# Seven block products for the value half of the second feed-forward, in 18 pairs of tiles

## The reference

```python
def conv_ffn(x, prev, w_up, conv_w, conv_b, w_down):
    L = x.shape[1]
    up = x @ w_up                                # 1024 -> 2 x 2816
    u, val = up[..., :D_FF], up[..., D_FF:]
    u_pad = jnp.concatenate([prev.astype(u.dtype), u], axis=1)
    c = conv_b
    for j in range(CONV_W):
        c = c + conv_w[j] * u_pad[:, j:j + L]
    h = jax.nn.gelu(c, approximate=True) * val
    return h @ w_down, u_pad[:, -(CONV_W - 1):]  # 2816 -> 1024
```

## Time and profile before

| what | value |
|---|---|
| runs | 2580.8, 2582.04, 2585.12 us |
| profiled execution | 2581.35 us, of which the span is 2579.5 us |
| TensorE busy | 2452.5 us (95%), 15399 matmuls |
| VectorE busy | 1614.0 us (63%) |
| ScalarE busy | 1149.6 us (45%) |
| GpSimd busy | 44.0 us (2%), DMA issues only |
| granted TensorE clock, mean | 0.988 of full |

### The profile page before, as it was taken

One profiled execution on the slowest core, in us unless ns is written; L12 is line 12 of the kernel. 1 busy time (PEld: TensorE's weight loads), 2 busy tenths in 40 slices (PEclk: granted clock), 3 DMA queues, 4 the chain that ended last, 5 costly groups with the idle time before them and its releaser, 6 DMA issues. The chain is left out here.

```text
span 2579.5 us, 37702 instructions
## 1 busy us (share of the span) xinstructions
PE 2452.5 (95%) x15399; PEld 2142.2 (83%) x15399; DVE 1614.0 (63%) x2922; ACT 1149.6 (45%) x1822; POOL 44.0 (2%) x66
## 2 busy tenths in 40 slices
PE   7999999989999999999998999889999999999997
PEld 4777988877888889999996677767788889999996
DVE  5667576675765556665656655665766556655556
ACT  4655454554343334343336666664344333423333
POOL 0000000000000000000000000000000000000000
PEclk9999999999999999999999999989999999999998
DMA  4222223323433322422323242222332323332322
GB/s 159 66 67 90 82 85 102 125 100 96 153 104 123 102 90 92 138 82 90 109 77 106 83 130 63 80 75 83 111 131 92 104 92 98 99 116 82 97 85 97
DMA packets 83592, 255.18 MB, mean 99 GB/s; under 512 B 12963, under 2 KB 30540, under 8 KB 81484
## 3 DMA queue, kind: packets, MB, share of 16 engines
q1 hardware_dynamic: 64348, 202.45, 25.0%
q0 software_dynamic: 5792, 28.05, 3.4%
q10 hardware_dynamic: 13280, 22.28, 2.6%
HBM read 225.93 MB, written 26.74 MB: 98 GB/s over the span
## 5 line engine op out<-in xcount | busy, mean ns | idle before, releaser
L447 PE MATMUL banks<-act_hi,w_lo 128*128 128x272 f32 (+1 forms) x2952 | 973.4, 330 | 15.7 <-DVE act_lo L2301 6.7
L447 PE MATMUL banks<-act_hi,w_hi 128*128 128x272 f32 (+1 forms) x2952 | 960.2, 325 | 0.0
L447 PE MATMUL banks<-act_lo,w_hi 128*128 128x272 f32 (+1 forms) x2952 | 958.3, 325 | 0.0
L425 ACT ACTIVATE w_hi<-w_raw 128x1024 fp32r<-128x1024 f32 x366 | 380.8, 1055 | 690.8 <-PE banks L470 487.2
L430 DVE TENSOR_TENSOR w_lo<-w_raw,w_hi 128x1024 fp32r<-128x1024 f32 x366 | 442.9, 1222 | 365.4 <-ACT w_hi L425 365.0
L447 PEld LDWEIGHTS banks<-act_hi,w_lo 128*128 128x128 f32 x2952 | 558.7, 189 | 75.4 <-issue 20.6
L447 PEld LDWEIGHTS banks<-act_lo,w_hi 128*128 128x128 f32 x2952 | 559.4, 190 | 43.2 <-issue 1.7
L447 PEld LDWEIGHTS banks<-act_hi,w_hi 128*128 128x128 f32 x2952 | 558.2, 189 | 43.8
L482 DVE TENSOR_TENSOR acc<-acc,banks 128x272 f32<-128x272 f32 (+1 forms) x624 | 314.7, 518 | 190.8 <-PE banks L470 187.3
L470 PE MATMUL banks<-h_hi,w_lo 128*128 128x272 f32 (+1 forms) x1056 | 345.3, 327 | 22.2 <-DVE acc L482 12.8
L470 PE MATMUL banks<-h_hi,w_hi 128*128 128x272 f32 (+1 forms) x1056 | 343.4, 325 | 0.0
(11 more groups left out here) (242 smaller groups left out, 2581.2 us busy)
## 6 DMA issues: line engine op xcount, KB each, us to landing
w_raw<-wall SPq DMA_DIRECT2D x366, 512.0 KB, 3.6
normed<-h_scratch POOLq DMA_DIRECT2D x20, 352.0 KB, 4.2
h_scratch<-acc POOLq DMA_DIRECT2D x3, 2176.0 KB, 7.8
h_scratch<-acc POOLq DMA_DIRECT2D x3, 2048.0 KB, 7.6
gstates<-state ACTq DMA_DIRECT2D x4, 1024.0 KB, 6.4
gla_s<-gstates ACTq DMA_DIRECT2D x4, 1024.0 KB, 6.8
bias<-bias_scratch ACTq DMA_DIRECT2D x28, 128.0 KB, 2.6
bias_scratch<-bias_rows ACTq DMA_DIRECT2D x8, 383.0 KB
```

Source lines behind the costliest of these rows:

```text
L425: nc.scalar.activation(WH[:, b % RING], WR[:, b % RAW], ACT.Copy).then_inc(w_hi, 1)
L447: last = nc.tensor.matmul(PS[:, bank, 0:n], w, a[X][:, k, o:o + n], start=(k == 0 and first), stop=(k == KT - 1 and w is wh and a is AH))
```

## The change

For f = 2 and 3 and each group g >= 2 (tiles 4 to 21, nine pairs each, 18 in all) the value half of the two tiles is computed together as a product of 2 x 2 blocks by Winograd's form of Strassen's scheme: the outputs are two tiles by two halves of the tokens (256 or 272 columns each), the sum runs over two halves of the features (KH = 4 blocks each). Instead of eight block products there are seven (`pe_products`), each of 12 matmuls of 256 or 272 columns.

- **Weights.** A pair has eight names in the list: u, u, `va`, `vs`, `vb`, `v4` and two downs. `va` and `vb` are loaded, each one half of the features of both tiles; `vs` (two sums, full size) and `v4` (one sum, half size) are made by GpSimd from them (`gp_three_sums`, `gp_fourth_sum`, four additions or subtractions of 128 x 512 per pair). `va` and `vs` are rounded after the third sum. So ScalarE and VectorE handle 7.5 blocks a pair where there were 6; loads stay 6.
- **Activation sums.** Four sums and differences of quarters of the activations are made once per half by GpSimd (`gp_act_sums`: eight instructions of 128 x 4 x 256 or 272, after the attention's last downs for f=2, after the last product of f=2 for f=3). ScalarE rounds them (`sums_hi`, four) and VectorE takes their rests (`sums_lo`, four) in tile 3, ahead of the round behind `val` and ahead of `product`, respectively.
- **Outputs.** ScalarE copies product 1 out of PSUM, VectorE makes seven additions and subtractions (`read_products`: `early`, `even`, `odd_tile`), then multiplies both tiles in SBUF by the gelu.
- **Order.** In an even tile t >= 4 TensorE does `u` and at once the downs of the group before, in an odd one `u` and the seven products. VectorE makes the even tile's convolution, a weight rest and up to two norm steps between the additions of the downs.
- **Waits and tables.** `u` of an even tile waits for the seventh read of the pair before; `u` of tile 0 of f=3 for the last multiply of f=2. `Root` and the steps behind it come later by two tiles and more (tables `DVE_SEVEN`, `DVE_AMID`, `ACT_SEVEN`). The result stores of tile 8 (f=3) now come ahead of the gelu of an even tile that is followed by the downs. Some semaphores are merged.

```diff
+SEVEN = (2, 3)
+def seven(f, g):
+    return f in SEVEN and g >= 2
...
+            pe.wait_ge(w_lo, BLK["va", f, g] + 1)
+            product("va", 1, own(AH, 0, 0), own(AL, 0, 0), 2)
+            pe.wait_ge(t_lo, 4 * SEVEN.index(f) + 4)
+            product("va", 0, made(TH, 0), made(TL, 0), 3)
+            pe.wait_ge(w_lo, BLK["vs", f, g] + 1)
+            pe.wait_ge(u_ev, TILE[f, odd, 0] if X else TILE[f, odd - 1, 0])
+            product("vs", 1, made(TH, 1), made(TL, 1), 0)
+            pe.wait_ge(u_ev, TILE[f, odd, c - 1])
+            product("vs", 0, made(TH, 2), made(TL, 2), 1)
+            pe.wait_ge(w_lo, BLK["vb", f, g] + 1)
+            pe.wait_ge(vp_read, 8 * N - 7)
+            product("vb", 1, own(AH, 1, 0), own(AL, 1, 0), 2)
+            pe.wait_ge(vp_read, 8 * N - 6)
+            product("vb", 0, made(TH, 3), made(TL, 3), 0)
+            pe.wait_ge(w_lo, BLK["v4", f, g] + 1)
+            pe.wait_ge(vp_read, 8 * N - 5)
+            product("v4", 0, own(AH, 1, 1), own(AL, 1, 1), 3)
...
+            if t % 2 == 0 and seven(f, t // 2 - 1):
+                pe.wait_ge(vp_read, 8 * SEVENS[f, t // 2 - 1] - 1)
+            elif t == 0 and seven(f - 1, FG - 1):
+                pe.wait_ge(vp_read, 8 * SEVENS[f - 1, FG - 1])
+                pe.wait_ge(h_made, TILE[f - 1, FT - 1, len(CHUNKS[1 - X]) - 1])
...
+            def seven_tile(f, t):                      # VectorE
+                g = t // 2
+                if t % 2 == 0:
+                    far = 1 + f % 2
+                    amid = ffn_steps((DVE_AMID, DVE_AMID), f, t)
+                    conv_before(f, t)
+                    for m in range(8 * far):
+                        down_add(dve, f % 2, (f, g - 1), m, 4 + m % 4, False)
+                        if m == far:
+                            rest_after(dve, ("u", f, t))
+                        elif m == 2 * far:
+                            conv_first(f, t)
+                        elif m == 3 * far:
+                            conv_second(f, t)
+                        elif m in (5 * far, 6 * far) and len(amid) > m // far - 5:
+                            dve_step(dve, *amid[m // far - 5])
+                    for x in range(2):
+                        rest_after(dve, ("d", f, g - 1, x))
+                    return
+                for step in ffn_steps((DVE_FFN[0], DVE_SEVEN[0]), f, t):
+                    dve_step(dve, *step)
+                early, even, odd_tile = read_products(f, g)
+                rest_after(dve, ("u", f, t))
+                conv(f, t)
+                rest_after(dve, ("va", f, g))
+                early()
+                rest_after(dve, ("vs", f, g))
+                even()
+                odd_tile()
+                rest_after(dve, ("vb", f, g))
+                dve_ffn_lo(dve, f, t - 1)
+                rest_after(dve, ("v4", f, g))
+                dve_ffn_lo(dve, f, t)
...
                 if f % 2 or t:
                     rest_after(dve, ("val", f, t))
+                if f in SEVEN and t == 3:
+                    for i in range(4):
+                        sums_lo(f, i)
                 product(f, t)
...
+                if f in SEVEN and t == 3:              # ScalarE
+                    sums_hi(f)
+                act.wait_ge(val_full, VALS[f, t, n - 1])
                 if X or t:
                     round_after(act, ("val", f, t))
...
+        def gp_three_sums(gp, f, g):
+            N = SEVENS[f, g]
+            a, b = raw(BLK["va", f, g]), raw(BLK["vb", f, g])
+            c0, a0, d0 = a[:, 0:KH * P], a[:, KH * P:], b[:, 0:KH * P]
+            if N > 1:
+                gp.wait_ge(w_lo, LAST_V4[N] + 1)
+            raw_in(gp, BLK["va", f, g])
+            nc.gpsimd.tensor_tensor(VX[:, 0], a0, c0, ALU.add).then_inc(v_sum, 1)
+            raw_in(gp, BLK["vb", f, g])
+            gp.wait_ge(v_sum, 4 * N - 3)
+            nc.gpsimd.tensor_tensor(c0, c0, d0, ALU.add).then_inc(v_sum, 1)
+            gp.wait_ge(v_sum, 4 * N - 2)
+            nc.gpsimd.tensor_tensor(VX[:, 1], c0, a0, ALU.add).then_inc(v_sum, 1)
```

More of the change, by code:

```diff
@@ L96, in ffn_tile, with ffn_tile_pair, ffn_up @@
         put(("val", f, t), b + 1)
+    def ffn_tile_pair(f, g):
+        w0 = (W_F0, W_F1)[f // 2]
+        for what in ("va", "vs", "vb", "v4"):
+            put((what, f, g), w0 + 4 + 6 * (g - 1) + 1)
+    def ffn_up(f, t):
+        put(("u", f, t), (W_F0, W_F1)[f // 2] + 4 + 6 * (t // 2 - 1) + 4 * (t % 2))
     def ffn_downs(f, g):
@@ L412, in build @@
         TILE = tally([(f, t, c) for f in range(4) for t in range(FT) for c in range(len(CHUNKS[f % 2]))])
+        VALS = tally([(f, t, c) for f in range(4) for t in range(FT) if not seven(f, t // 2) for c in range(len(CHUNKS[f % 2]))])
+        SEVENS = tally([(f, g) for f in range(4) for g in range(FG) if seven(f, g)])
+        LOADED = [b for b in range(NW) if names[b][0] not in ("vs", "v4")]
+        RAWI = {b: r for r, b in enumerate(LOADED)}
         AQ = tally([(X, p, c) for X in range(2) for p in range(8) for c in range(len(CHUNKS[X]))])
@@ L1390, in pe_ffn_tile, with tokens, pe_products, product @@
                 project(pe, X, BLK["val", f, t], c, 2 + (t % 2 if n == 1 else c), val_full)
-        PE_NAMES = {t: (name,) for t, name in PE_FFN.items()}
+        PE_NAMES = [{t: (name,) for t, name in table.items()} for table in PE_FFN]
+        def tokens(X, j):
+            n = WX[X] // 2
+            return slice(j * n, j * n + n)
+        def pe_products(pe, f, g):
+            X, n = f % 2, WX[f % 2] // 2
+            odd, N = 2 * g + 1, SEVENS[f, g]
+            c = len(CHUNKS[X])
+            def product(block, half, hi, lo, bank):
+                s = BLK[block, f, g] % RING
+                for k in range(KH):
+                    wh, wl = (W[:, s, (half * KH + k) * P:(half * KH + k + 1) * P] for W in (WH, WL))
+                    for x, (w, a) in enumerate(((wl, hi), (wh, lo), (wh, hi))):
+                        last = nc.tensor.matmul(PS[:, bank, 0:n], w, a(k), start=(k == 0 and x == 0),
+                                                stop=(k == KH - 1 and x == 2))
+                last.then_inc(vp_full, 1)
+            def own(A, half, j):
+                return lambda k: A[X][:, half * KH + k, tokens(X, j)]
+            def made(A, i):
+                return lambda k: A[:, i, k, 0:n]
+            pe.wait_ge(w_lo, BLK["va", f, g] + 1)
[15 more added lines that the diff above has]
+            product("v4", 0, own(AH, 1, 1), own(AL, 1, 1), 3)
         def pe_ffn_downs(pe, f, g):
@@ L1483, in dve_ffn @@
             for f, t in ffn_tiles(l):
-                for step in ffn_steps(DVE_FFN[0], f, t):
+                if seven(f, t // 2):
+                    seven_tile(f, t)
+                    continue
+                for step in ffn_steps((DVE_FFN[0], DVE_SEVEN[0]), f, t):
                     dve_step(dve, *step)
@@ L2419, in _ @@
             for i, X in PASSES[1:]:
-                for y in range(4):
+                f = {(3, 1): 2, (4, 0): 3}.get((i, X))
+                for y in range(2):
                     h_load(gp, i, X, y)
-                if i < 4:
+                if f is None:
+                    for y in range(2, 4):
+                        h_load(gp, i, X, y)
+                else:
+                    gp_act_sums(gp, f)
+                    for g in range(2, FG):
+                        gp_three_sums(gp, f, g)
+                        if g == 2:
+                            h_load(gp, i, X, 2)
+                        gp_fourth_sum(gp, f, g)
+                        if g == 2:
+                            h_load(gp, i, X, 3)
+                        if g == 3 and i < 4:
+                            h_store(gp, i, X)
+                if f is None:
                     h_store(gp, i, X)
```

236 lines of the change are left out of this document (204 added, 32 removed).

## The result

The kernel after the change takes 2599.68 us (median of four runs, 2597.86 to 2606.74) against 2583.28 us for the kernel before on the same chip: ratio 1.0069, 95% interval 1.0048 to 1.009. It is slower by 16 us. The forecast was 2585.0 us with a range to 2598: the sign "slower" had 0.37, and the time lies 1.7 us outside the range. The profiled execution took 2600.46 us, its span is 2598.6 us, 19.1 us over that of before.

What follows compares the result with a forecast made beforehand. It took TensorE's matmuls to bound the kernel: 2581.35 - 24.3 (fewer columns) - 1.8 (stalls) + 24.0 (edges) + 5 (GpSimd) = 2584.3 us, with the runs' median 0.7 above, 2585.0 us; range 2566 to 2598.

Steps and rivals of the forecast that it cites:

- What bounds the kernel: Both halves' plain pairs are bound by TensorE's matmuls; the f=3 chain's 3.2 us between runs beside TensorE's work.
- two stalls: Two f=3 pairs, ending at 2241.83 and 2316.83, lose 0.7 and 1.1 us before; the change removes 1.8 us.
- What it removes: Seven block products for eight save 10.7 us at f=2 and 13.6 us at f=3, 24.3 us together, plus 1.8 us.
- rival D: The 256-column matmuls cost as much as 272-column ones: 5.4 us more, 2590 us; no chance of its own.
- Plain pairs: The added VectorE work costs plain pairs nothing: 32.4 us at f=2, 35.4 us at f=3.
- rival C: The odd tile's tail is 0.7 us late in each of 18 pairs, 13 us: 2598 us; chance 0.08.
- Edges (1) to (3): TensorE stalls before tile 4's downs, 7.3 us (f=2) and 8.5 us (f=3), then a lower clock, 4 us together.
- Rival A: The gain comes through, with no tile 3 stalls or clock loss: faster, 2560 to 2572 us; chance 0.27.
- Edge (4): Tile 11 of f=2: the second root delays ScalarE's copy and rounds, so `u` waits 1.5 us.
- edge (5): The two seams: `u` of f=3 tile 0 waits 1.3 us, the last downs wait 1.4 us more.
- my 5 us: GpSimd's activation sums, mainly the first batch at the start of f=2, hold VectorE up: 5 us of 0 to 13.
- Rival B: GpSimd's batches hold VectorE up in full in the first 20 us of f=2: slower, 2593 us; chance 0.20.

Runs made afterwards that it cites:

- e11: Kernel before, with VectorE's first four additions of the downs moved ahead of the product where a half has two chunks: 2568.53 us, ratio 0.9951.
- e1: Changed kernel, with the activation sums' four roundings and four rests moved from tile 3 into the downs of tile 2: 2580.51 us, ratio 0.999.
- e4: Changed kernel, with the residual stream's store of half 1 issued one pair later: 2594.24 us, ratio 1.0045.
- e2: Changed kernel, with GpSimd's eight activation-sum instructions per half cut to 16 columns each, sums not computed: 2581.53 us, ratio 0.9993.
- e3: Changed kernel, with each of GpSimd's sixteen batch instructions issued as four of a quarter of the columns: 2588.23 us, ratio 1.0021.
- e5: Changed kernel, with GpSimd's batch for f=3 started at the first unit of the last downs of f=2: 2593.23 us, ratio 1.0037.

## Why the prediction was wrong

**What bounds the kernel.** Right that matmuls do; wrong in that no wait was in the f=3 pairs. I read the "3.2 us between" of the chain as work beside TensorE. Its step at L470 that began 72 matmuls before the end of the downs was the pause of 0.67 us that e11 removed. The gain was so 5.1 us larger than forecast over nine pairs and two stalls, and it hid part of the loss.

**What it removes.** Right: 118.0 ns for 256 columns (118.6 forecast), so rival D is out, and -11.2 us at f=2 (-10.7). At f=3 the count was right, the base was not. Nine plain pairs and the two stalls would be 21.9 us there; 20.5 came, and most of the difference is the first pair behind tile 4 (35.8 us, 2271.48 to 2307.26), which was not tried apart.

**Plain pairs.** Right: 32.31 us (32.4). The tail fits; rival C is out. 34.71 us at f=3 (35.4) for the reason above.

**Edges (1) to (3).** Right: 6.99 and 8.3 us (7.3 and 8.5), the clock 2.1 us each (2 each), 19.5 us in all. e1 shows that nothing else was behind them: taken out, they gave 19.2 us. Rival A is out.

**Edge (4).** 2.1 us where 1.5 stood. This and the 0.9 us of tiles 5 to 7 were not tried apart.

**The store.** 5.4 us, not in the sum. I costed the change's DMA only as "loads stay 6". In the seven-product order GpSimd issues the store behind its fourth sum, which VectorE had held to 4.61 us, and the store met the loads of the downs. e4 won 4.0 us back there.

**GpSimd and edge (5): the step that failed.** At the start of f=2 my 5 us were near the 5.8 measured, and e2 shows that they are the batch's, but the working behind them was wrong and the match is luck. I halved a bound of 9.8 us; in the trace VectorE's instructions grew by 10.6 us, and 5.8 of them reached the end. "Nothing is in reserve" was also read from the wrong place: the 3.96 of 4.00 us of the earlier trace rows are those from 1800 on, while from 1783 to 1797 VectorE was busy for 5.0 of 14 us. At the seam I gave 1.3 us, with "0 and about 3" for GpSimd as bounds, and it cost 12.5; e2 leaves 1.7 of them. The time that VectorE would need for the eight itself was no bound. The price is per VectorE instruction, one GpSimd instruction of 2.4 us each time, so a batch costs most where VectorE has many short instructions on the path. The seam is such a place: two rests and two h_lo stand ahead of the last downs, in a list that I had summed at 4.5 us myself. Rival B named the cause and its sign, but put its place at the start of f=2, with 3 us at most for the seam, and took its price (2593) from that same bound. The Trainium skill's rule ("SBUF — State Buffer", section "SBUF: two separate sides"), which the traces of after, e3 and e5 bear out, gave in my estimate up to 18 us for the first batch and a result near 2598, closer than the forecast; both batches together cost 5.8 + 10.8 us here, most of it at the seam, which that estimate left out.

**The end.** 2.5 us (1.4): TensorE waits 4.0 us ahead of the last downs where it waited 3.13, 0.9 us more. The other 1.5 us are the first 72 matmuls of these downs, which take 10.65 us where they took 9.11, at a lower granted clock; the windows of after and of before:

```profile
2565.10:2576.00 10.90, 10.88 (x74) 10.86 (x75) 6.10 (x16) 2.64 (x4) 0.00 (x0) 0.84 0.41 174
...
2547.60:2557.00 9.40, 9.39 (x74) 9.36 (x75) 6.15 (x16) 2.63 (x4) 0.00 (x0) 1.00 0.51 213
```

The prediction had a clock term behind the two waits at tile 4 and none here.

**Balance.** The seam is 11.2 us of the 15.9 us between the sums, the store 5.4, the small edges with the execution's own start 4.9, and the pairs give 5.6 back. With the seam at its forecast cost the time would have been near 2588 us, inside the range (an estimate: 2599.7 - 11.2).

## What to carry to other kernels

When work moves to GpSimd, count VectorE's instructions that read only SBUF while it runs, and add one GpSimd instruction's length for each that is on the path; put long GpSimd instructions beside VectorE work that reads PSUM, or cut them. For every instruction put into an in-order queue ask whose date stands behind it: four roundings and four subtractions ahead of one product, once per half, cost 19.2 us (e1), more than the count of matmuls was to save in nine pairs of f=3 (13.6). And look into a stretch that seems back to back for a short pause that repeats; 0.67 us per pair, in f=1 and f=3, was worth 12 us here.

## What the runs showed of the hardware

- GpSimd adds 128 x 512 in 1.29 us and 128 x 1024 in about 2.4 us when VectorE leaves it alone; with VectorE in turns up to 4.61 us (128 x 512) and 3.4 us (128 x 1088).
- A VectorE instruction that reads SBUF alone can wait for a whole GpSimd instruction, even a copy of two columns (from 0.16 to 2.50 us). One with an operand in PSUM isn't delayed (0.69 us for 128 x 512, e5).
- Quartering the GpSimd instructions quarters the delay of each (2.3 to 0.55 us), and makes the batch longer (23 to 35 us at f=2, 24 to 34 us at the seam).
- Behind an idle time of 7 us the granted clock was 0.50 for 4 us and 0.94 on average over the next 13 us. In the last downs it was 1.00 behind an idle time of 3.13 us (before) and 0.84 behind one of 4.0 us (after); at the start of f=2 it was 0.51 for 3 us behind one of 2.65 us (before). So the length of the idle time alone did not decide it.
